# The FFN in two phases: a seven-product down projection whose first weight sum, too, is made by an adding DMA

## The reference, cut to what matters

```python
xm = rmsnorm(h, p['norm_mlp_g'])                                # (t, 2048)
h = h + jnp.square(jax.nn.relu(xm @ p['w_up'])) @ p['w_down']    # w_up (2048, 8192), w_down (8192, 2048)
y = rmsnorm_final(h)
```

## Time and profile before

| | us |
|---|---|
| median of 3 runs | 2770.23 (2767.11 to 2770.42) |
| the profiled execution: its time | 2766.59 |
| its span, first to last instruction | 2764.8 |
| TensorE busy | 2731.3 |
| VectorE busy | 1513.4 |
| ScalarE busy | 910.8 |
| GpSimd busy | 618.6 |
| granted TensorE clock, mean | 0.992 |

### The profile page before, as it was taken

One profiled execution on the slowest core, in us unless ns is written; L12 is line 12 of the kernel. 1 busy time (PEld: TensorE's weight loads), 2 busy tenths in 40 slices (PEclk: granted clock), 3 DMA queues, 4 the chain that ended last, 5 costly groups with the idle time before them and its releaser, 6 DMA issues.

```text
span 2764.8 us, 51075 instructions
## 1 busy us (share of the span) xinstructions
PE 2731.3 (99%) x21572; PEld 2616.8 (95%) x21572; DVE 1513.4 (55%) x2063; ACT 910.8 (33%) x1187; POOL 618.6 (22%) x292
## 2 busy tenths in 40 slices
PE   9999999999999999999999999999999999999998
PEld 7999998777999988789999999999999999999998
DVE  4687936666323334422474655746557465564665
ACT  5221125535222211222332432514325143251442
POOL 2545434675443322344200000000000000000000
PEclk9999999999999999999999999999999999999999
DMA  6734345555532666543327666666665665656653
GB/s 191 142 101 103 103 129 163 169 176 162 169 91 76 206 198 198 161 133 114 109 83 215 166 173 181 159 187 165 173 180 157 191 162 170 179 157 197 162 143 109
DMA packets 576409, 428.92 MB, mean 155 GB/s; under 512 B 36041, under 2 KB 493615, under 8 KB 574767
## 3 DMA queue, kind: packets, MB, share of 16 engines
q1 hardware_dynamic: 500152, 308.70, 38.8%
q10 hardware_dynamic: 72027, 102.69, 12.3%
q0 software_dynamic: 4032, 14.68, 2.8%
HBM read 357.78 MB, written 53.84 MB: 149 GB/s over the span
## 4 chain that ended last, share of the span: by engine, by line
PE 86%; issue 6%; POOL 4%; DVE 2%; ACT 1%; DMA 1%; SPq 0%; POOLq 0%; DVEq 0%; ACTq 0%
PE lin L1654 32%; PE lin L2259 27%; PE aux L2224 17%; PE lin L2224 3%; POOL wlo L932 3%; POOL wlo L890 2%; PE aux L1976 1%; PE aux L1931 1%; PE lin L1871 1%; PE aux L1922 1%; PE lin L1744 1%; DVE rot L2311 0%; PE aux L1821 0%; PE aux L1817 0%; DMA piece<-in_cache_mem_v 0%
## 5 line engine op out<-in xcount | busy, mean ns | idle before, releaser
L890 POOL TENSOR_TENSOR wlo<-raw,whi 128x1024 fp32r<-128x1024 f32 x176 | 433.6, 2467 | 658.9 <-ACT whi L976 467.3
L2259 PE MATMUL lin<-fl,whi 128*128 128x260 f32 x2048 | 577.3, 282 | 0.0
L2259 PE MATMUL lin<-fh,wlo 128*128 128x260 f32 x2048 | 577.2, 282 | 0.0
L2259 PE MATMUL lin<-fh,whi 128*128 128x260 f32 x2048 | 576.8, 282 | 0.0
L1486 ACT ACTIVATE whi<-raw 128x1024 fp32r<-128x1024 f32 x212 | 224.2, 1057 | 507.6 <-DVE hr L3150 400.1
L2259 PEld LDWEIGHTS lin<-fh,wlo 128*128 128x128 f32 x2048 | 385.8, 188 | 0.0
L2259 PEld LDWEIGHTS lin<-fh,whi 128*128 128x128 f32 x2048 | 385.2, 188 | 0.0
L2259 PEld LDWEIGHTS lin<-fl,whi 128*128 128x128 f32 x2048 | 384.9, 188 | 0.0
L3041 DVE TENSOR_TENSOR wlo<-raw,whi 128x1024 fp32r<-128x1024 f32 x240 | 292.6, 1219 | 29.8 <-ACT whi L1486 29.8
L947 POOL DMA_DIRECT2D sums<-raw x28 | 24.4, 871 | 1242.8 <-DMA sums<-in_w_up 1242.8
L3146 DVE TENSOR_TENSOR part<-lin,rB 128x520 f32<-128x520 f32 x128 | 89.5, 699 | 383.0 <-PE lin L2259 376.5
(11 more groups left out here) (483 smaller groups left out, 6836.4 us busy)
## 6 DMA issues: line engine op xcount, KB each, us to landing
raw<-in_w_up SPq DMA_DIRECT2D x128, 512.0 KB, 4.4
raw<-in_w_down SPq DMA_DIRECT2D x128, 512.0 KB, 4.3
hr<-hscr ACTq DMA_DIRECT2D x128, 260.0 KB, 3.4
raw<-in_w_in SPq DMA_DIRECT2D x60, 512.0 KB, 3.8
hscr<-hr ACTq DMA_DIRECT2D x112, 260.0 KB, 2.1
raw<-in_w_out SPq DMA_DIRECT2D x32, 512.0 KB, 3.9
raw<-in_w_q SPq DMA_DIRECT2D x32, 512.0 KB, 4.0
piece<-in_cache_mem_k SPq DMA_DIRECT2D x32, 512.0 KB, 6.0
```

Of the source, the lines that this page charges most:

```text
L890: pool.tensor_tensor(wlo[:, slot, :], raw[:, slot % 2, :], whi[:, slot, :].bitcast(F32), ALU.subtract).then_inc(s.w_lo, 1)
L2259: mm = pe.matmul(lin[:, 2 * i + f, 0:HALF], w, x[:, kk, HALF * f:HALF * f + HALF], start=(first and m == 0 and part == 0), stop=(last and ...
```

## The change

The FFN is split in two phases. First all of the up projection: 4 direct pairs and 28 quads (`Q`), one after the other. Each finished quad, and each direct pair, is scaled by rB, its blocks' sums are made (`hidden_sums`), and ScalarE's queue stores seven blocks of it to a new DRAM tensor `hidd`, 910 KB. Then the down projection, in 8 passes `p` over 1024 hidden features. A pass has 4 groups (`G` counts all 32), each of 512 output features, and each group is seven products of 24 matmuls (`down_product`). The hidden blocks of a pass (7 of 520 KB) are loaded by SP during the pass before and split by ScalarE and VectorE (`block_hi`, `block_lo`). The weights' sums are the same three on VectorE and the same S1 by SP's load and GpSimd's adding DMA, but the products take the weights in another order (`DOWN_SOURCE`). The four results of a group (`corner_of`) go to one of two buffers `cbuf`, and GpSimd adds them to `hscr` in DRAM with an adding DMA of 1040 KB (`add_out`), for the first 28 groups. In the last pass `hscr` is loaded (`load_last`) and the sum is made in SBUF. A weight block of the down projection is loaded in runs of 1 KB instead of 512 B. The order of the products, the banks and the waits of the up quads stay, apart from the parts below. `N_GROUP` is 32, `GROUPS` 4, `N_QUAD` 28.

```diff
+    hidd = nc.dram_tensor("hidd", [N_CHUNK, P, 7, 4, HALF], F32, kind="Internal").ap()
+        DOWN_SOURCE = (A11, S1, S2, A12, A21, A22, S2)
+        BANK_X, BANK_Y = lin[:, 0:2, 0:HALF], lin[:, 2:4, 0:HALF]
+        BANK_W, BANK_Z = aux[:, 0:2, 0:HALF], aux[:, 2:4, 0:HALF]
+        DOWN_BANK = (BANK_X, BANK_Y, BANK_X, BANK_W, BANK_X, BANK_Z, BANK_Y)
...
+            def load_block(p, k):
+                if p > 0:
+                    sp.wait_ge(s.blk_lo, BLK_LO + 7 * (p - 1) + k + 1)
+                if p < 2:
+                    if p == 0 and k < 2:
+                        sp.wait_ge(s.pe_unit, U_UP)
+                        sp.wait_ge(s.s_sum, 2 * KF)
                     else:
+                        sp.wait_ge(s.pe_unit, up_n(N_QUAD - 1, ((0, 0, 0, 0, 1, 1, 2), (3, 3, 4, 4, 5, 5, 2))[p][k]) + 1)
                 else:
+                    sp.wait_ge(s.pe_unit, down_n(GROUPS * (p - 1) - 1, k) + 1)
+                for i in range(2):
+                    sp.wait_ge(st_out[i], ST_OUT[i] + 32 * (QUADS // 2) * (p + 1))
+                sp.dma_start(xbl[p % 2][k][:].bitcast(F32), hidd[p, :, HID_BLOCK[k], :, :]).then_inc(blk_in[k], 16)
+            def load_down(G, r):
+                i, j = ((0, 0), (1, 1), (1, 0), (0, 1))[r]
+                if G == 0:
+                    Q = N_QUAD
+                    sp.wait_ge(*((s.s1_add, 16 * Q) if r == 1 else (s.s_sum, 2 * KF + 3 * (Q - 1) + (2, 0, 2, 3)[r])))
+                    sp.wait_ge(s.w_lo, up_n(Q - 1, (0, 1, 3, 5)[r]) + 1)
+                else:
+                    sp.wait_ge(*((s.s1_add, 16 * (N_QUAD + G)) if r == 1 else (s.s_sum, SUMS + 3 * (G - 1) + (2, 0, 2, 3)[r])))
+                    sp.wait_ge(s.w_lo, down_n(G - 1, (0, 5, 4, 3)[r]) + 1)
+                p, g = G // GROUPS, G % GROUPS
+                sp.dma_start(RAW4[r].rearrange("p (k n) -> p k n", n=256),
+                             kp(io["w_down"])[:, KF * p + j:KF * p + KF:2, 512 * g + 256 * i:512 * g + 256 * i + 256]
+                             ).then_inc(raw4_in[r], 16)
+            def load_down_first(G):
+                if G == 0:
+                    sp.wait_ge(s.s_sum, 2 * KF + 3 * N_QUAD - 2)
+                    sp.wait_ge(s.w_lo, up_n(N_QUAD - 1, 4) + 1)
+                else:
+                    sp.wait_ge(s.s_sum, SUMS + 3 * (G - 1) + 1)
+                    sp.wait_ge(s.w_lo, down_n(G - 1, 1) + 1)
+                p, g = G // GROUPS, G % GROUPS
+                sp.dma_start(S1.rearrange("p (k n) -> p k n", n=256),
+                             kp(io["w_down"])[:, KF * p:KF * p + KF:2, 512 * g + 256:512 * g + 512]).then_inc(s.glu_in, 16)
...
+            for G in range(N_GROUP):
+                p, g = G // GROUPS, G % GROUPS
+                if p + 1 < N_CHUNK:
+                    for k in ((0, 1, 2), (3, 4), (5, 6), ())[g]:
+                        load_block(p + 1, k)
+                if G + 1 < N_GROUP:
+                    load_down_first(G + 1)
+                    for r in (0, 3, 2, 1):
+                        load_down(G + 1, r)
...
+            def add_out(G):
+                g = G % GROUPS
+                pool.wait_ge(s.c_done, C_DONE + 4 * G + 4)
+                pool.dma_start(hscr[:, 4 * g:4 * g + 4, :], cbuf[G % 2][:], accum_op=ALU.add, max_dma_last_dim=4160).then_inc(c_add[G % 2], 16)
+            for G in range(N_GROUP):
+                pool.wait_ge(s.glu_in, 32 + 16 * (N_QUAD + G + 1))
+                pool.wait_ge(s.raw1, ARRIVED[1] + 16 * (N_QUAD + G + 1))
+                pool.dma_start(S1, A22, accum_op=ALU.add).then_inc(s.s1_add, 16)
+                if 0 < G <= N_GROUP - GROUPS:
+                    add_out(G - 1)
...
+            def high(n, src):
+                act.wait_ge(s.pe_unit, n - 3)
+                act.activation(whi[:, n % 4, :], src, ACT.Copy).then_inc(s.w_hi, 1)
...
+            def hi_down(G, k):
+                if k in (0, 3, 5):
+                    arrived({0: 0, 3: 3, 5: 1}[k], N_QUAD + G + 1)
+                elif k == 1:
+                    act.wait_ge(s.s1_add, 16 * (N_QUAD + G + 1))
+                else:
+                    act.wait_ge(s.s_sum, SUMS + 3 * G + {2: 1, 4: 2, 6: 3}[k])
+                high(down_n(G, k), DOWN_SOURCE[k])
...
+            def store(R):
+                c, kk = R // QUADS, R % QUADS
+                act.wait_ge(s.t_done, T_DONE + R + 1)
+                dma(hidd[c, :, 0, kk, :], st[:, R % 2, 0, :], st_out[R % 2])
+                dma(hidd[c, :, 1:7, kk, :], st[:, R % 2, 2:8, :], st_out[R % 2])
...
+            def copied(G, k, buf):
+                act.wait_ge(s.pe_unit, down_n(G, k) + 1)
+                if G > 0:
+                    act.wait_ge(s.c_done, C_DONE + 4 * (G - 1) + {0: 1, 2: 4, 4: 3}[k])
+                act.activation(buf[:], BANK_X, ACT.Copy).then_inc(s.copied, 1)
...
+            def group(G):
+                p, g = G // GROUPS, G % GROUPS
+                blocks = [7 * (p + 1) + k for k in ((0,), (1, 2), (3, 4), (5, 6))[g]] if p + 1 < N_CHUNK else []
+                end = p == N_CHUNK - 1
+                hi_down(G, 2)
+                if G == 0:
+                    block_hi(5)
+                    even(N_QUAD - 1)
+                if end:
+                    load_last(g)
+                copied(G, 0, p1d)
+                hi_down(G, 3)
+                if G == 0:
+                    block_hi(6)
+                if G == 1:
+                    store(QUADS + N_QUAD - 1)
+                if end and g > 0:
+                    last_half(2 * g - 2)
+                hi_down(G, 4)
+                for j in blocks[0:1]:
+                    block_hi(j)
+                copied(G, 2, u2d)
+                hi_down(G, 5)
+                for j in blocks[1:2]:
+                    block_hi(j)
+                if end and g > 0:
+                    last_half(2 * g - 1)
+                hi_down(G, 6)
+                copied(G, 4, u3d)
+                if G + 1 < N_GROUP:
+                    hi_down(G + 1, 0)
+                    hi_down(G + 1, 1)
             def up_tile(p, i):
                 act.wait_ge(s.tile_free, 2 * p + (O_MLP + i + 1))
                 act.activation(hsqF[:], upr[:], ACT.Square).then_inc(s.up_sq, 1)
             def combined(k):
             act.wait_ge(s.xs_st, 64 + 16 * KT)
...
+            def down_product(G, k, first, last):
+                n, p = down_n(G, k), G // GROUPS
+                pe.wait_ge(s.w_lo, n + 1)
+                if G % GROUPS == 0:
+                    pe.wait_ge(s.blk_lo, BLK_LO + 7 * p + k + 1)
+                hi, lo = xbh[p % 2][k], xbl[p % 2][k]
+                for pr in range(2):
+                    for kk in range(4):
+                        wh = whi[:, n % 4, 256 * kk + P * pr:256 * kk + P * pr + P]
+                        wl = wlo[:, n % 4, 256 * kk + P * pr:256 * kk + P * pr + P]
+                        for part, (w, m) in enumerate(((wh, hi), (wh, lo), (wl, hi))):
+                            mm = pe.matmul(DOWN_BANK[k][:, pr, :], w, m[:, kk, :], start=(first and kk == 0 and part == 0),
+                                           stop=(last and kk == 3 and part == 2), skip_group_check=True)
+                mm.then_inc(s.pe_unit, 1)
+            def group(G):
+                if G > 0:
+                    pe.wait_ge(s.copied, COPIED + 3 * G)
+                down_product(G, 0, True, True)
+                if G > 0:
+                    pe.wait_ge(s.c_done, C_DONE + 4 * G)
+                else:
+                    pe.wait_ge(s.q_ev, 5 * N_QUAD)
+                down_product(G, 1, True, True)
+                pe.wait_ge(s.copied, COPIED + 3 * G + 1)
+                down_product(G, 2, False, True)
+                if G == 0:
+                    pe.wait_ge(s.up_sq, act_n(N_QUAD - 1, 4))
+                down_product(G, 3, True, True)
+                pe.wait_ge(s.copied, COPIED + 3 * G + 2)
+                down_product(G, 4, False, True)
+                down_product(G, 5, True, True)
+                pe.wait_ge(s.c_done, C_DONE + 4 * G + 2)
+                down_product(G, 6, False, True)
...
+            def up_scaled(p, i):
+                v.wait_ge(s.up_sq, 4 * p + 2 * i + 2)
+                if i == 0:
+                    slot_stored(p)
+                v.tensor_tensor(st[:, p % 2, 2 * i:2 * i + 2, :], halves(hsqF[:]), halves(rB[:]), ALU.mult).then_inc(s.hid_lo, 1)
...
+            def hidden_sums(R):
+                b = st[:, R % 2, :, :]
+                tt(b[:, 4:6, :], b[:, 1:4:2, :], b[:, 0:2, :], ALU.subtract)
+                tt(b[:, 6, :], b[:, 3, :], b[:, 4, :], ALU.subtract)
+                tt(b[:, 7, :], b[:, 6, :], b[:, 2, :], ALU.subtract, s.t_done)
...
+            def down_sum(G, k):
+                a = 16 * (N_QUAD + G + 1)
+                if k == 2:
+                    v.wait_ge(s.raw0, ARRIVED[0] + a)
+                    v.wait_ge(s.s1_add, a)
+                    v.wait_ge(s.w_lo, (down_n(G - 1, 6) if G > 0 else up_n(N_QUAD - 1, 6)) + 1)
```

(67 more changed lines are left out.)

576 lines of the change are left out of this document (258 added, 318 removed).

## The result

The changed kernel takes 2954.34 us in the median of four runs (2949.34 to 2966.95), the kernel before 2770.32 beside them (2767.11 to 2772.57): a ratio of 1.0672, 95% interval 1.0637 to 1.0707. That is 184 us slower; the profiled execution took 2955.45. Slower was the side forecast; the time is far outside the range.

A forecast was written before the change was run, and what follows sets the result against it. The prediction took the FFN to be bound by TensorE's number of matmuls. It summed 2766.6 - 90.6 (fewer matmuls) + 86.7 + 10.0 (down groups) + 10.4 (other edits) = 2783 us, put at 2785 for the median; range 2738 to 2860.

The forecast's parts named there:

- The loop: Down groups: each hangs on the one before through A22's load and the adding DMA; 23.3 us against TensorE's 20.09.
- its seven steps: Down group: bank copy, low part, load issue, A22's load, adding DMA, VectorE's queued work, products 1 and 2; 22.2 us.
- E: The end of product 2 of a down group, from which the forecast counted its times.
- step (6): Down group: after the awaited sum, VectorE does low part 1, another sum and corner 3: 4.1 us, plus 0.15 for TensorE.
- step (7): Down group, end of the circle: products 1 and 2 and the last matmul's tail take 5.9 us.
- the term: Down phase: loss over TensorE's pace, 86.7 us for the first 27 groups that follow a group, 10.0 for the last four.
- it still fits, by 1.8: Up quads: VectorE's work behind sum S2 ends 1.8 us before product 2 begins; 3 us put for the phase (0 to 25).
- start, junction and tail: Start of the up phase, passage from up to down, and end: 2, 4.4 and 1 us lost.
- (a): Rival, down groups: the loop turns without delay from other transfers, T 22.2 us, 2753 us in all; chance 0.28.
- (b): Rival, down groups: no loop, load and addition take 6.4 us together, TensorE stays full, 2686 us; chance 0.07.
- (c): Rival, down groups: the addition into DRAM holds the engines before A22 lands; T 26.5 gives 2869 us; chance 0.23.
- T: The period of a down group: 23.3 us forecast, between 21.7 and 27.

The follow-up runs named there:

- experiment 9: Changed kernel with two S1 places (up), two A22 places (down), their loads first, next addition ahead of the DRAM one, corner 3 ahead of sum 3: 2701.72 us.
- Experiment 8: Changed kernel with 24 thrown-away matmuls before product 1 of down groups after the first, and the addition into DRAM carrying one of four tiles: 2891.05 us.
- experiment 3: Changed kernel, down groups only: two A22 places, its load earlier, next weight sum issued ahead of the addition into DRAM, hidden blocks loaded last: 2786.49 us.
- experiment 5: Changed kernel, down groups only: VectorE makes S1 by a plain addition again, without first load and adding DMA: 2810.01 us.
- experiment 1: Changed kernel with 24 thrown-away matmuls on TensorE before product 1 of each down group after the first: 2940.48 us.
- experiment 2: Changed kernel, up phase only: S1 has two places used in turn, and S1's first load and A22's load stand first: 2873.53 us.
- experiment 6: Changed kernel, up phase only: stores of the hidden blocks issued half a quad later, still one S1 place: 2883.92 us.

## Why the prediction was wrong

**Right.** The matmuls (672 a pass, 20.09 us a group where nothing holds it: 20.24 between corners 3 in experiment 9). The loop, its seven steps and where TensorE stands: before product 1, once a group, released by corner 3, with VectorE caught on the adding DMA 31 times (137.5 us). In the group shown high and low part end 2.9 after E (2.95 forecast), and step (6) takes 4.16 until TensorE starts (4.1 + 0.15). Load and addition take 10.5 us in the mean and GpSimd's issue 0.55 more, 11.0 together; the forecast had 4.4 + 4.7 + 0.3 + 0.8 = 10.2 for them, so 0.8 too little. The addition into DRAM, taken at most at 11.4, has 11.0.

**Wrong, step (7): "Products 1 and 2 and the last matmul's tail: 5.9".** They take 7.78 in the mean. The forecast itself said that TensorE would stand for some 3 us in each group (it was 3.7), and went on at 2.4 GHz behind the stop. All stages of the earlier trace rows had a granted clock of 1.00, so no row that I had read showed what a stop does, and I did not ask. The trace of the kernel before could have told, ahead of the FFN, where TensorE stood for 3.16 us until 698.52:

```profile
695.40:698.50 3.10, 0.00 (x0) 0.00 (x0) 3.00 (x4) 2.18 (x5) 2.35 (x1) 1.00 0.40 86
698.80:702.10 3.30, 3.30 (x17) 3.30 (x17) 1.80 (x3) 0.00 (x0) 0.00 (x0) 0.50 1.00 419
```

In a loop this is paid in full: 23.3 + 1.9 for the half clock + 0.8 for load and addition = 26.0, for 25.90 measured. Over 31 groups that is some 59 and 25 us; the term was 96.7 (86.7 and 10.0) and measured 180.1 (161.0 and 19.1), 83.4 more. The last pass, whose groups issue neither loads of blocks nor an addition into DRAM (one of group 27 still runs at its start), shows the same: 24.87 us a group for the 22.6 forecast, and 24.26 in its last two steps. Experiment 8 has 23.5 in the group shown and 23.84 in the mean with the clock held (and a small transfer into DRAM), where TensorE alone needs 22.97; experiments 3 and 5 show that the half clock goes with the stops. The loop at full clock with the full transfer was not measured by itself, since in experiment 1 some groups still stopped; so the two shares hold for the chain of this one kernel, and are not what taking away either alone would give.

A rule of the Trainium skill speaks of this (TensorE: Matmul & The Clock Gate, HAM oscillation): where each tile ends in a wait for a DMA, the half clock comes back in every tile, and the loop should be arranged anew. This trace agrees: stops of 1.8 to 6.8 us before product 1, where TensorE waits for VectorE behind two DMAs, and the lower level in 30 of 31 groups. It would have been the rule to weigh against the change.

**Wrong, the up phase: "28 quads now run back to back at 20.09 ... it still fits, by 1.8 ... I put 3 us for the phase (0 to 25)".** I checked whether S2's sum would be in time for product 2, once, within a quad, and asked only there what a slow addition does. I didn't follow S1's buffer round to its next load, as I did in the down groups. Before, that loop stood at 19.19 of 20.09, with 0.9 us of slack where I had seen 1.8; and the addition took the 7 us that I named as the danger in most quads (median 7.8), because the stores travel beside it: in the quad shown ScalarE's queue issues them at 1743.04, GpSimd the addition at 1744.97. So the failed step is the wait for S1's next load, which the forecast did not have: 72.9 us instead of 3. Experiments 2 and 6 each take it away, by another end of the loop. With the stores moved the phase has 20.20 a quad.

**Small: start, junction and tail.** 18.9 for 7.4 forecast; not taken apart by experiment. Another 7.6 lie ahead of the FFN.

2783 + 69.9 + 83.4 + 11.5 + 7.6 = 2955.4, the profiled execution. Slower was forecast, with 0.53, and for a loop that is there, which isn't luck; the size was missed in both phases. Of the rivals, (a) and (b) are refuted (a period of 25.90, load and addition at 11.0 together), and (c)'s mechanism is real but small: three quarters of the transfer are worth 1.0 us a group, where it asked for some 4. The range (2738 to 2860) took the half clock at nothing and the up phase at 25 at most. With the down groups' miss alone the sum would be 2783 + 83.4 = 2866, just past its end, with the up phase's alone 2853, inside; the two together left it. That the bounds of T, 21.7 to 27, hold the measured 25.90 is luck: their upper part stood for a slow addition into DRAM, and what filled it was mostly the half clock.

## What to carry to other kernels

For each buffer that is loaded anew in every iteration, walk the circle from its last reader through the load, what is computed from it and whoever is queued behind that, back to the last reader, and compare its length with the bound engine's period; do it for the parts of the code that are not changed too, with every transfer at its time beside the new traffic. Where the circle is longer, price the stop of TensorE as well as the half clock that comes with it. The cure is more room in the circle (a second place, an earlier load), or a store moved out of the addition's way. It need not be a faster transfer: with the room, the adding DMAs of the down groups were slower and the kernel 2.4% faster than before.
